# The sample's attention cut into head pairs and run inside the next pair's projections, with its products on VectorE, and eight instead of six convolution taps in the first stage

## What is computed

```
xn = RMSNorm(x);  q, k, v, glu, gates = split(xn @ w_in)
q, k = RMSNorm per head of 64;  3 groups x 8 heads, (window, dilation) = (128,1), (512,4), (2048,16)
prompt: banded attention per group
sample: per row b, head h, group g: s = q . k_cache rows at distances 0, d, 2d, ... and the new key
        softmax over all 128 + 128 + 67 keys of the three groups together, o = p @ v
u = glu_a * sigmoid(glu_b);  c = causal depthwise conv over 31 taps of u + bias
merged = sigmoid(g_A) * (o @ w_attn_out) + sigmoid(g_C) * (silu(LayerNorm(c)) @ w_conv_out)
h = x + merged @ w_o;  y = h + W2 relu(W1 RMSNorm(h))^2
also written: the keys and values of the prompt, the caches shifted by one row, the conv state
```

## Time and profile before

| | |
|---|---|
| median of 3 runs | 1095.64 us (1094.68 to 1095.77) |
| profiled execution | 1095.88 us, span of its instructions 1094.0 us |
| TensorE clock granted, mean | 0.970 of full speed |
| busy: PE / VectorE / ACT / POOL | 1032.0 / 638.4 / 418.9 / 147.3 us |
| first stretch, to the first GLU unit | 0 to 33.8 us |
| GLU units | 33.8 to 138.5 us together with the first two projections of pair 0 |
| four pairs, to their last matmul | to 485.6 us |
| channel gate, conv-out and attention-out units | 485.6 to 666.5 us |
| `w_o` and MLP | 666.5 us to the end |

### The profile page before, as it was taken

One profiled execution on the slowest core, in us unless ns is written; L12 is line 12 of the kernel. 1 busy time (PEld: TensorE's weight loads), 2 busy tenths in 40 slices (PEclk: granted clock), 3 DMA queues, 4 the chain that ended last, 5 costly groups with the idle time before them and its releaser, 6 DMA issues.

```text
span 1094.0 us, 21484 instructions
## 1 busy us (share of the span) xinstructions
PE 1032.0 (94%) x8290; PEld 1013.3 (93%) x8290; DVE 638.4 (58%) x768; ACT 418.9 (38%) x604; POOL 147.3 (13%) x163
## 2 busy tenths in 40 slices
PE   2999999999999999997677999999999999999998
PEld 2999999999999999997667999999999999999998
DVE  3666688787867878877786634554432224443221
ACT  4333344434434344433663143345441114543221
POOL 3000000310030040037256012200000000000000
PEclk8899999999999999999788899999999999999999
DMA  6233594394386368237566612334443444344442
GB/s 177 78 96 95 194 363 128 123 323 130 97 294 214 115 216 279 67 107 270 128 209 155 233 59 61 113 125 136 144 144 124 135 145 144 122 137 144 145 154 68
DMA packets 172456, 169.33 MB, mean 155 GB/s; under 512 B 7386, under 2 KB 162170, under 8 KB 169687
## 3 DMA queue, kind: packets, MB, share of 16 engines
q1 hardware_dynamic: 163271, 138.49, 39.8%
q0 software_dynamic: 9120, 29.95, 8.3%
HBM read 159.12 MB, written 64.79 MB: 205 GB/s over the span
## 4 chain that ended last, share of the span: by engine, by line
PE 82%; DVE 5%; DMA 4%; issue 3%; ACT 3%; POOL 1%; SPq 1%; DVEq 0%; ACTq 0%; POOLq 0%
PE ps L714 71%; DMA w_raw<-in_w_conv_out_dram 2%; PE ps L615 1%; ACT w_high L1019 1%; DVE w_low L1319 1%; PE ps L651 1%; PE ps L559 1%; PE ps L567 1%; PE ps L818 1%; PE ps L654 1%; DVE c_low L1196 1%; DMA chan_rows<-in_norm_g_dram 1%; DVE ln_sum L1442 1%; PE ps L597 1%; POOL gate_a L1721 1%
## 5 line engine op out<-in xcount | busy, mean ns | idle before, releaser
L1319 DVE TENSOR_TENSOR w_low<-w_raw,w_high 128x1024 fp32r<-128x1024 f32 x152 | 202.2, 1330 | 312.9 <-ACT w_high L1019 308.1
L714 PE MATMUL ps<-x_high,w_high 128*128 128x260 f32 x1600 | 327.3, 286 | 1.9 <-ACT glu_sig L949 1.0
L714 PE MATMUL ps<-x_high,w_low 128*128 128x260 f32 x1600 | 322.6, 283 | 0.0
L1019 ACT ACTIVATE w_high<-w_raw 128x1024 fp32r<-128x1024 f32 x152 | 160.9, 1058 | 421.5 <-PE ps L714 390.0
L714 PE MATMUL ps<-x_low,w_high 128*128 128x260 f32 x1600 | 322.1, 283 | 0.0
L714 PEld LDWEIGHTS ps<-x_high,w_high 128*128 128x128 f32 x1600 | 247.8, 189 | 5.4 <-ACT glu_sig L949 2.0
L714 PEld LDWEIGHTS ps<-x_low,w_high 128*128 128x128 f32 x1600 | 247.1, 189 | 0.0
L714 PEld LDWEIGHTS ps<-x_high,w_low 128*128 128x128 f32 x1600 | 247.0, 189 | 0.0
L1192 DVE SCALAR_TENSOR_TENSOR conv<-u_in,chan,conv x240 | 167.0, 743 | 6.6 <-DVE conv L1192 5.1
L714 PE MATMUL ps<-hid_high,w_high 128*128 128x260 f32 x512 | 103.7, 284 | 0.0
L714 PE MATMUL ps<-hid_high,w_low 128*128 128x260 f32 x512 | 103.1, 283 | 0.0
(11 more groups left out here) (238 smaller groups left out, 1100.8 us busy)
## 6 DMA issues: line engine op xcount, KB each, us to landing
w_raw<-in_w_in_dram SPq DMA_DIRECT2D x68, 512.0 KB, 4.4
w_raw<-in_w_ff_dram SPq DMA_DIRECT2D x64, 512.0 KB, 4.0
out_dram<-in_cache_v_dram SPq DMA_DIRECT2D x64, 256.0 KB, 6.7
out_dram<-in_cache_k_dram SPq DMA_DIRECT2D x64, 256.0 KB, 4.0
out_dram<-in_cache_k_dram SPq DMA_DIRECT2D x8, 1022.0 KB, 7.0
out_dram<-in_cache_v_dram SPq DMA_DIRECT2D x8, 1022.0 KB, 7.2
kbuf<-in_cache_k_dram POOLq DMA_DIRECT2D x2, 2048.0 KB, 14.4
qbuf<-new_qkv POOLq DMA_DIRECT2D x4, 1024.0 KB, 7.5
```

The source lines that it names most:

```text
L714: mm = pe.matmul(out[:, h, :], w[:, k, n0:n0 + P], x[:, k0 + k, h * HT:(h + 1) * HT], start=(first and k == 0 and n == 0), stop=(last and ...
L1019: act.activation(w_high[a % 2][:, :, :], w_raw[a % 2][:, :, :], ACT.Copy).then_inc(cast_done, 1)
L1319: dve.tensor_tensor(w_low[a % 2][:, :, :], w_raw[a % 2][:, :, :], w_high[a % 2][:, :, :].bitcast(F32), ALU.subtract).then_inc(split_done, 1)
```

## The change

- The sample's attention is cut by head pair. Slice t (two heads, 8 rows, three groups) runs inside pair t+1, slice 3 inside the channel gate and conv-out stages.
- Its buffers: `sa`, four slots of 128 x 8 x 128 values (1024 a partition) instead of `kbuf`, `qbuf`, `kbuf2` (4096 a partition each).
- All products are done by VectorE: per slice three key products with three reductions (`sample_keys`), the maximum, the normalisation, three value products and two additions (`sample_values`).
- PE: three score transposes in the middle of projection 6, three probability transposes after the third part of projection 7, eight one-column matmuls after projection 9. For slice 3: after channel gate units 5 and 7 and after conv-out unit 2.
- POOL: the loads are cut to 512-byte rows and moved into the pairs (`first_keys`, `first_queries`, `later_loads`: 12 transfers a slice). The stores of the new rows come first in a pair's stores, and `first_queries` waits for their landing before the value stores are issued.
- `GLU_TAPS` 8; `TAP_SLOTS` sums to 46 and is laid out anew; `Fori` loops over the pairs are written out.
- `x_prompt` and `gate_rows` are fetched earlier.

```diff
-GLU_TAPS = 6
+GLU_TAPS = 8
-TAP_SLOTS = (3, 3, 3, 3, 3, 3, 3, 2, 2, 5, 6, 3, 4, 3, 4)
+TAP_SLOTS = (4, 0, 1, 4, 1, 3, 3, 3, 3, 3, 3, 4, 5, 4, 5)
+BANK6 = ("sum0", "sum1", "sum2", "sum3", "sum4", "st", "sum5", "tk0", "tk2", "tv0", "tv2", "o0", "vs", "o1")
+BANK7 = ("sum0", "sum1", "sum2", "sum3", "sum4", "sum5", "tk1", "sp", "mt0", "tv1", "nq", "nk", "mt1", "nv")
...
+        def sample_probs_turn(pe, t):
+            pe.wait_ge(s_pn, t + 1)
+            pe.wait_ge(free7, 1 + use_no(BANK7, t + 1, "sp"))
...
+        def sample_value_sums(pe, t):
+            pe.wait_ge(v_sum, 5 * t + 5)
+            pe.wait_ge(free6, 1 + use_no(BANK6, t + 1, "vs"))
+            for b in range(TS):
+                mm = pe.matmul(ps[:, 6, b:b + 1], sa[:, 2, b, :], ones[:, 0:1], start=True, stop=True)
...
+                        if k == 4:
+                            sample_scores_turn(pe, t - 1)
...
             parts(7, 0, 3)
+            if t:
+                sample_probs_turn(pe, t - 1)
             scores_far(0)
...
             parts(9, 4, 8)
+            if t:
+                sample_value_sums(pe, t - 1)
             turn_max(1)
...
+                if j == 5:
+                    pe.wait_ge(ln_rs, 1)
+                    sample_scores_turn(pe, 3)
+                if j == 7:
+                    sample_probs_turn(pe, 3)
...
+        def sample_keys(dve, t, g):
+            n = SROWS[g]
+            k_slot, q_slot = (0, 2, 0)[g], (1, 3, 1)[g]
+            dve.wait_ge(slot_in[k_slot], 16 * (5 * t + 1, 2 * t + 1, 5 * t + 3)[g])
+            dve.wait_ge(slot_in[q_slot], 16 * (3 * t + 1, 2 * t + 1, 3 * t + 3)[g])
+            dve.tensor_tensor(sa[0:n, k_slot, :, :], sa[0:n, k_slot, :, :], sa[0:n, q_slot, :, :], ALU.mult).then_inc(kq_done, 1)
+            dve.wait_ge(kq_done, 3 * t + g + 1)
+            dve.tensor_reduce(s_score[0:n, g, :], by_head(k_slot, n), AX.X, ALU.add).then_inc(s_red, 1)
...
+                if t and i in (1, 2, 4):
+                    sample_keys(dve, t - 1, i // 2)
+                if t and i == 5:
+                    sample_max(dve, t - 1)
                 taps()
             norm(5)
             next_split(6)
+            if t:
+                sample_norm(dve, t - 1)
             taps()
...
             shifts(0)
+            if t:
+                sample_values(dve, t - 1, 0)
             taps()
             next_split(8)
+            if t:
+                sample_values(dve, t - 1, 1)
             taps()
...
+                if j == 2:
+                    sample_keys(dve, 3, 0)
+                    sample_keys(dve, 3, 1)
                 if j == 3:
+                    sample_keys(dve, 3, 2)
                     dve.wait_ge(ln_rs, 1)
...
+                if j == 6:
+                    sample_max(dve, 3)
+                if j == 7:
+                    sample_norm(dve, 3)
...
+            def later_loads(t):
+                pool.wait_ge(s_red, 3 * t + 1)
+                load_queries(t, 2, 1)
+                load_cache(t, cache_k, krow, 2, 0)
+                pool.wait_ge(s_red, 3 * t + 2)
+                load_cache(t, cache_v, vrow, 0, 2)
+                load_cache(t, cache_v, vrow, 1, 3)
+                pool.wait_ge(s_red, 3 * t + 3)
+                load_cache(t, cache_v, vrow, 2, 0)
...
+            for t in range(4):
+                if t:
+                    later_loads(t - 1)
+                first_keys(t)
+                pool.wait_ge(free6, 2 + use_no(BANK6, t, "tv2"))
+                pool.wait_ge(free7, 2 + use_no(BANK7, t, "nv"))
+                for n in range(3):
+                    pool.dma_start(scratch[n][:, :, col], new_tok[:, n, :, :]).then_inc(new_stored, 16)
                 pool.dma_start(rows(pk[0])[0][:, col], k_tok[:, NB - 1, 0, :]).then_inc(kv_stored, 16)
                 for g in (1, 2):
                     pool.dma_start(rows(pk[g])[0].rearrange("(j r) c -> j r c", r=NB)[:, :, col], k_tok[:, :, g, :]).then_inc(kv_stored, 16)
+                first_queries(t)
                 for hh in range(2):
...
-            product(0, 0)
-            load_queries(1, 0)
-            product(0, 1)
```

More of the change, by code:

```diff
@@ L91, with bank_uses, use_no @@
 U_FF = U_WO + 8
-GLU_TAPS = 6
-BANK6 = ("sum0", "sum1", "sum2", "sum3", "sum4", "sum5", "tk0", "tk2", "tv0", "tv2", "o0", "o1")
-BANK7 = ("sum0", "sum1", "sum2", "sum3", "sum4", "sum5", "tk1", "mt0", "tv1", "nq", "nk", "mt1", "nv")
-N6, N7 = len(BANK6), len(BANK7)
+GLU_TAPS = 8
+BANK6 = ("sum0", "sum1", "sum2", "sum3", "sum4", "st", "sum5", "tk0", "tk2", "tv0", "tv2", "o0", "vs", "o1")
+BANK7 = ("sum0", "sum1", "sum2", "sum3", "sum4", "sum5", "tk1", "sp", "mt0", "tv1", "nq", "nk", "mt1", "nv")
+SAMPLE = ("st", "sp", "vs")
+def bank_uses(order, t):
+    return [name for name in order if (t > 0 or name not in SAMPLE) and (t < 4 or name in SAMPLE)]
+def use_no(order, t, name):
+    return sum(len(bank_uses(order, s)) for s in range(t)) + bank_uses(order, t).index(name)
 TURNS = ("sum0", "sum1", "sum2", "sum3", "sum4", "sum5", "tk0", "tk1", "tk2", "tv0", "tv1", "tv2", "nq", "nk", "nv")
-TAP_SLOTS = (3, 3, 3, 3, 3, 3, 3, 2, 2, 5, 6, 3, 4, 3, 4)
+TAP_SLOTS = (4, 0, 1, 4, 1, 3, 3, 3, 3, 3, 3, 4, 5, 4, 5)
 S_AT = (0, 512, 896, 1408)
@@ L538, in project @@
                     pe.wait_ge(norm_done, cnt(6, i - 2))
+                if i == 6 and t:
+                    for k in range(KT):
+                        if k == 4:
+                            sample_scores_turn(pe, t - 1)
+                        mm = unit(U_QKV + PER_T * t2 + i, 2 * PER_T, tt, pair(i % 3), x_high, x_low, part=k)
+                    mm.then_inc(unit_done, 1)
+                    return
                 unit(U_QKV + PER_T * t2 + i, 2 * PER_T, tt, pair(i % 3), x_high, x_low).then_inc(unit_done, 1)
@@ L754, in _ @@
             pe.wait_ge(head_ones_done, 3)
-            for tt in range(2):
-                for t2 in range(2):
-                    qkv_pair(pe, unit, tt, t2)
+            for t in range(4):
+                qkv_pair(pe, unit, t)
             pe.wait_ge(exp_done, 4 + 4 * 8)
@@ L794, in _ @@
                      ready=(lambda k: pe.wait_ge(c_low_done, k + 1)) if j == 0 else None).then_inc(unit_done, 1)
[L795 to L823, removed]
+                if j == 2:
+                    sample_value_sums(pe, 3)
+            pe.wait_ge(free6, 2 + use_no(BANK6, 4, "vs"))
             for j in range(4):
@@ L990, in act_pair @@
             first_keys(0)
+            if t:
+                sample_probs(act, t - 1)
             value_copy(1)
@@ L1063, in _ @@
             act.preload_act_table_set("natural_log_exp_and_others")
-            with act.Fori(0, 2) as tt:
-                for t2 in range(2):
-                    act_pair(act, cast, done, tt, t2)
+            for t in range(4):
+                act_pair(act, cast, done, t)
             def ln_square(k):
@@ L1421, in _ @@
             dve.tensor_tensor(sc, sc, bias_b, ALU.add).then_inc(sconv, 1)
-            with dve.Fori(0, 2) as tt:
-                for t2 in range(2):
-                    dve_pair(dve, split, tt, t2)
+            for t in range(4):
+                dve_pair(dve, split, t)
             for j in range(8):
@@ L1624, in _ @@
                                        v_tok[:, g * NB:(g + 1) * NB, 2 * hh, :]).then_inc(kv_stored, 16)
-                for n in range(3):
-                    pool.dma_start(scratch[n][:, :, col], new_tok[:, n, :, :]).then_inc(new_stored, 16)
                 pool.wait_ge(gate_copied, 2 * t + 4)
```

273 lines of the change are left out of this document (131 added, 142 removed).

## The result

| | before | after |
|---|---|---|
| median | 1095.35 us (1094.36 to 1095.77, 7 runs) | 1100.10 us (1097.82 to 1105.79, 7 runs) |
| ratio | 1 | 1.0043, 95% interval 1.0030 to 1.0057 |
| profiled execution | 1095.88 us | 1105.79 us |

The change makes the kernel slower by 4.7 us; 1084.5 was forecast, with a range up to 1097. The times of the changed kernel spread over 8 us where those of before spread over 1.4, and the profiled execution is the longest of the seven, 5.7 above their median. Shares by stage are therefore read from it with care, and the experiments are compared by their medians.

The account below looks back on a forecast made before the run. The prediction took TensorE to bound the pairs (89.3 of 90 us busy), with gains only in the 180.9 us after. From 1095.88, 2.1 - 0.5 + 12.0 + 3.6 - 6.5 - 21.9 = -11.2 gave 1084.7, stated as 1084.5, range 1074 to 1097.

Parts of the forecast that it names:

- the paragraph on DMA: Pairs: the sample's loads, some 1.8 MB a pair, 5.0 us of backlog, just fit; nothing charged, up to 4 in the range.
- lead of 5.8: Pairs: a weight is asked for about a unit ahead, 5.8 us, less the cast, to cover the backlog of loads.
- Rival C: Pairs: loads of the sample delay weights, 4 us a pair more, 1096; no chance of its own.
- Both signs of being wrong: Pairs 1 to 3 longer by over 7.7 us, or weights' landings lengthening in the pairs, would show the forecast wrong.
- +4.0 a pair: Pairs 1 to 3: TensorE's transposes and one-column products, small waits and a later `c_sum`; +12.0 us, bounds 2.1 and 13 each.
- +3.6 for the mean: TensorE's wait for `c_sum` before the mean, 2.07 us, grows as POOL's queries wait for new-row stores; bounds 0 and 5.4.
- -0.5 for the unrolled loops: Between pairs 1 and 2: the jump back that cost VectorE and TensorE a wait goes; -0.5 us, bounds -0.5 and 0.
- Rival A: Pairs: VectorE's order, not its sum, decides; late splits make TensorE stand, 13 us a pair, 1111 in all; chance 0.12.
- Value sums: TensorE: eight one-column products a slice, 16 records at 11 per us, 1.45 us; at clock 1.00 instead of 10.86 us.
- First stage: GLU stage and its end: two more taps a tile cost +0.2, the last tile's uncovered taps 1.9; +2.1 us.
- Mean to conv-out 0: From the mean to conv-out unit 0: 67.6 us becomes 61.1, third key slice on the path; -6.5 us, bounds -12 and 0.
- Conv-out 0 to `w_o`: From conv-out unit 0 to `w_o`: 103.2 us becomes 81.3 without weight waits and long value sums; -21.9, bounds -22.5 and -10.

Follow-up runs that it names:

- e1: Changed kernel with the 64 cache copies of 256 KB that SP issues in the pairs issued in the MLP instead, one a unit: 1081.69 us, ratio 0.9884.
- e10: Changed kernel with each load of cache rows and queries taking four of eight sample rows, 1.95 MB a slice instead of 3.9: 1084.72 us, ratio 0.9906.
- e5: Control: the kernel before, with the same 64 cache copies moved from the pairs to the MLP as in e1: 1095.30 us, ratio 1.000.
- e2: Changed kernel with VectorE's key products, value products and additions of the sample on one of eight rows, reductions and transfers whole: 1093.50 us, ratio 0.9982.
- e9: Changed kernel with the 2 MB of `x_prompt` fetched in four pieces behind conv-out units 0 to 3, cache copies left in the pairs: 1094.73 us, ratio 0.9994.
- e8: Kernel of e6 with VectorE's third key slice of the last sample slice moved behind the second half of the LayerNorm's scaling: 1075.60 us, ratio 0.9809.
- e6: Changed kernel with both the edit of e1 and that of e9: 1077.22 us, ratio 0.9823.
- e7: Kernel of e6 with the pairs' eight one-column value sums spread as 3, 3 and 2 behind the first gate unit's first three parts: 1083.28 us, ratio 0.9884.

## Why the prediction was wrong, step by step

- **The step that failed** is the paragraph on DMA: "some 1.8 MB a pair" and "It just fits; I charge nothing". The bytes were mis-sized: 3.9 MB a slice by the rows after, and the shapes in the diff say so too (nine loads of up to 128 x 1024 values). At the forecast's own 361 GB/s that is 10.9 us of backlog instead of 5.0, against its lead of 5.8. What the runs showed in its place: DMA engines full for 46 us around the head of a pair (share 1.03), weights that land in 13.5 us instead of 5.9, and a cost of about 6 us a pair (e1: 18.4 us for three). Rival C had the mechanism, at "4 a pair more" and with no chance of its own. Both signs of being wrong that the prediction named came: pairs longer by over 7.7 us, and longer landings.
- **The sum of that paragraph** would have had the wrong sizes even with the right bytes. Landings grew by 7.6 us with the whole load and by 2.4 with half of it, not by 10.9 and 5.4. And a weight may come later than 5.8 us after its issue: the one of 244.71 came after 13.72 and cost 2.36, so some 11 would have done there (an estimate from these two numbers).
- **With half the loads,** about the 1.8 MB that the forecast assumed, e10 measured 1084.7. That this is the forecast's 1084.5 is in part luck: it holds an unpriced 5.4 for `x_prompt` (below) and 2 for its own start, and its pairs with the mean's wait took 4.7 less than forecast.
- The rule of the Trainium skill that was weighed there ("DMA: Bandwidth & Descriptors", Queues, rings and completion order: engines take turns between queues by packets) pointed this way: POOL's loads don't wait behind SP's. The trace agrees in so far as weights of SP's queue went from 5.9 to 13.5 us in the same stretch as POOL's bytes came in, and to 8.3 with half of them. The turns themselves no run shows, and the halving of SP's share that the prediction drew from them doesn't come out over the stretch as a whole: from 220 to 266 us SP's queue moved 10.98 MB and POOL's 4.04.
- **Pairs without the collision:** +4.0 a pair was forecast with +3.6 for the mean and -0.5, +15.1 in all. e1 has +3.9, +3.1 and +3.6 with the mean's wait in it, 10.7. VectorE's forecast of 83.5 us was 82.0; the eleven instructions, put at 12.4 us, come to 13.2 by the rows that it names. The mean's wait was oversized: 2.5, not 5.7. The new rows land in 1.8 us where they stand now, not in the 6.0 of the earlier trace rows; that this is the reason was not tested. The -0.5 for the unrolled loops isn't shown to be the loop's: e5 keeps the loops, and its pair 1 has no such wait and takes 89.43 us.
- **Rival A**, VectorE's order, is a part of it but not the main cause: e2 took 7.4 us a pair off VectorE and gained 6.6 in all.
- **Value sums:** 1.45 a slice was near for the last slice at full clock (1.84). In the pairs the forecast left out what it had itself read from the earlier trace rows, that the clock falls in such a stretch: pair 1 ran at 0.53 from 309 to 315. In e1 with the same sums it fell in one pair of three, from 301 to 305.
- **First stage:** +2.1 forecast, +2.8 measured (2.24 us of wait instead of 0.50); near, and for the reason given. Pair 0's +1.5 behind it is a spell at half clock that was not counted.
- **Mean to conv-out 0:** -6.5 forecast, -4.2 measured. Two errors of opposite signs (and the terms written down come to 60.7, not 61.1, which would be -6.9). The earlier fetch of `x_prompt`, named in the change, was not priced: it cost 5.4 (e9). And the chain was too long: without that fetch the stage gives about -9 (mean to conv-out 60.4 in e9 against 69.65), because the third key slice is not on the path (e8). That TensorE waits about 10 there came true only without that fetch (11); in the changed kernel it waits 16.0.
- **Conv-out 0 to `w_o`:** -21.9 forecast, -22.6 measured. The reading of the earlier trace rows, that POOL's products hold up VectorE, held: in the channel gate stage after, without them, splits take 1.22 and 1.23 us and three `c_low` 1.91.

Either of the two errors alone would have left the time within the range that was given: 1094.7 without the early `x_prompt` (e9), 1081.7 without the collision (e1). With both out of the way, e6 shows what the rest of the change is worth: 1077.2, some 7 below the forecast. e1, e6, e7 and e8, which leave nothing out, are all faster than both kernels.

## What to carry to other kernels

When transfers are moved, write down their bytes one by one and set the sum against what the engines have free in the stretch where they land (here a share of 0.81 before, over 46 us). Full engines don't show as waits as long as every load comes in time: before, TensorE waited for nothing from 414 to 420 us at a share of 1.02. In the changed kernel they show as short waits of TensorE for VectorE, with the late weight three steps behind. Price each DMA that the diff moves, also one that it moves merely to have it early. A control on the old kernel (e5) tells a collision from a burden.

## What the runs showed of the hardware

- The cost of the loads is not in proportion to their amount: with half of the set the pairs are as long as in e1, and the whole set costs 15 us more (1084.72 against 1100.10). That only what goes beyond the lead of the weights costs time fits the landings (8.3 us without a wait, 13.5 with waits); no run lies between.
- The same wait of 2.24 us ahead of pair 0 was followed by a granted clock of 0.52 from 142 to 145 us in the changed kernel and by 1.00 in e1. Windows of after, then of e1:

```profile
142.00:145.00 3.00, 3.00 (x16) 3.00 (x16) 3.00 (x5) 1.49 (x3) 0.45 (x1) 0.52 1.66 587
```

```profile
141.00:146.00 5.00, 4.79 (x40) 4.80 (x41) 4.97 (x9) 1.49 (x3) 0.90 (x2) 1.00 1.17 412
```

Of eight profiles with this wait of 2.23 or 2.24 us six show the fall, e1 and e9 do not. Why, stays open; a spell of this kind costs 1.5 to 3.5 us, so these may be a part of the spread of the times.
